# A fused encoder layer on one core: input projections in matmuls of 512 columns, and a last norm that is begun before the last expert's rows are in

## The reference, cut to what matters

```python
h = layer_norm(concat([meta, x]), ln_in_g, ln_in_b)        # 16 + 256 rows of 1024
proj = h @ w_in                  # q 256, k 256, v 512, og 512, a1 16, z 512, xbc 1024, dt 8
# GLA heads on q, k, v; SSD heads on conv(xbc), dt; outputs gated by silu(og), silu(z)
h1 = layer_norm(alpha * h + mix @ w_out, ln1_g, ln1_b)
# 32 experts, top 4 of each token; d_model = d_ff = 1024
hid = clamped_swiglu(xb @ w_gate[e] + b_gate[e], xb @ w_up[e] + b_up[e])
yb = (hid @ w_down[e] + b_down[e]) * gate
out = layer_norm(alpha * h1 + segment_sum(yb), ln2_g, ln2_b)   # 256 rows
```

## Time and profile before

| | |
|---|---|
| median of 3 runs | 1058.77 us (1058.34 to 1059.03) |
| the profiled execution | 1058.86 us, span of its instructions 1057.0 us |
| PE busy | 1021.6 us (97%) |
| DMA | 426.21 MB, mean 403 GB/s |
| VectorE, ScalarE, GpSimd busy | 228.6, 143.9, 29.7 us |
| mean granted TensorE clock | 0.991 |

### The profile page before, as it was taken

One profiled execution on the slowest core, in us unless ns is written; L12 is line 12 of the kernel. 1 busy time (PEld: TensorE's weight loads), 2 busy tenths in 40 slices (PEclk: granted clock), 3 DMA queues, 4 the chain that ended last, 5 costly groups with the idle time before them and its releaser, 6 DMA issues.

```text
span 1057.0 us, 12137 instructions
## 1 busy us (share of the span) xinstructions
PE 1021.6 (97%) x5116; PEld 449.5 (43%) x5116; DVE 228.6 (22%) x495; ACT 143.9 (14%) x348; POOL 29.7 (3%) x50
## 2 busy tenths in 40 slices
PE   8999999999999999999999999999999999999997
PEld 7888764333333333333333333333333333333332
DVE  5453572111111111111111112211111111111112
ACT  3312331111111111011110111111111110011102
POOL 1230100000000000000000000000000000000000
PEclk9999999999999999999999999999999999999999
DMA  9894689999999999999999999999999999999995
GB/s 314 273 410 192 201 327 410 428 428 435 429 429 435 432 425 433 435 436 424 430 435 436 424 422 436 432 430 426 435 434 428 428 435 435 430 425 427 428 418 236
DMA packets 40011, 426.21 MB, mean 403 GB/s; under 512 B 6922, under 2 KB 19347, under 8 KB 23204
## 3 DMA queue, kind: packets, MB, share of 16 engines
q1 hardware_dynamic: 37940, 424.12, 95.6%
q10 hardware_dynamic: 2032, 1.53, 0.6%
HBM read 424.59 MB, written 1.05 MB: 403 GB/s over the span
## 4 chain that ended last, share of the span: by engine, by line
PE 72%; DMA 26%; ACT 1%; DVE 0%; issue 0%; SPq 0%; POOL 0%; DVEq 0%; POOLq 0%; ACTq 0%
PE bank L1200 30%; DMA ring<-in_moe_w_up 18%; PE bank L1251 15%; DMA ring<-in_moe_w_gate 8%; PE bank L1180 4%; PE bank L1172 4%; PE bank L856 3%; PE bank L871 2%; PE bank L1046 2%; PE bank L1034 1%; PE bank L988 1%; PE bank L1242 1%; PE bank L1120 1%; PE bank L949 1%; PE bank L1054 1%; PE bank L1220 1%
## 5 line engine op out<-in xcount | busy, mean ns | idle before, releaser
L1200 PE MATMUL bank<-ring,arena 128*64 128x512 f32 x1988 | 447.5, 603 | 23.8 <-DMA ring<-in_moe_w_up 20.3
L1200 PEld LDWEIGHTS bank<-ring,arena 128*64 128x64 f32 x1988 | 142.5, 139 | 298.7 <-issue 257.7
L1251 PE MATMUL bank<-ring,arena 128*64 128x512 f32 x1024 | 226.8, 595 | 1.5 <-issue 1.5
L1251 PEld LDWEIGHTS bank<-ring,arena 128*64 128x64 f32 x1024 | 71.5, 137 | 151.7 <-issue 150.2
L1641 DVE COPY arena<-bank 128x512 f32<-128x512 f32 x32 | 22.1, 692 | 326.0 <-PE bank L1251 326.0
L741 ACT ACTIVATE arena<-arena 128x512 f32<-128x512 f32 x32 | 20.1, 629 | 451.1 <-DVE arena L1628 451.1
L1180 PE MATMUL bank<-arena 64*128 64x512 f32 x256 | 72.0, 640 | 0.9 <-DVE arena L1641 0.9
L1172 PEld LDWEIGHTS bank<-arena 128*128 128x128 f32 x480 | 58.8, 196 | 22.8 <-issue 22.8
L1635 DVE TENSOR_SCALAR arena<-bank 128x512 f32<-128x512 f32 x32 | 22.1, 692 | 210.3 <-PE bank L1200 210.3
L752 ACT ACTIVATE arena<-bank 128x512 f32<-128x512 f32 x32 | 19.1, 597 | 337.4 <-PE bank L1242 337.4
L1172 PE MATMUL bank<-arena 128*128 128x128 f32 x480 | 64.5, 288 | 0.0
(11 more groups left out here) (281 smaller groups left out, 511.6 us busy)
## 6 DMA issues: line engine op xcount, KB each, us to landing
ring<-in_moe_w_down SPq DMA_DIRECT2D x25, 4096.0 KB, 29.6
ring<-in_moe_w_gate SPq DMA_DIRECT2D x24, 4096.0 KB, 25.4
ring<-in_moe_w_up SPq DMA_DIRECT2D x24, 4096.0 KB, 28.2
ring<-in_moe_w_gate SPq DMA_DIRECT2D x10, 2048.0 KB, 22.6
ring<-in_moe_w_up SPq DMA_DIRECT2D x10, 2048.0 KB, 15.2
ring<-in_moe_w_down SPq DMA_DIRECT2D x10, 2048.0 KB, 17.4
ring<-in_w_in SPq DMA_DIRECT2D x12, 1024.0 KB, 11.8
ring<-in_moe_w_gate SPq DMA_DIRECT2D x8, 1024.0 KB, 17.2
```

What stands on the lines that cost most here:

```text
L1200: ins = mm(b[h * SL:(h + 1) * SL, :], (xA[pp], xB)[q][:, k, par * SL:(par + 1) * SL], columns(unit_at(m, kt), h), start=False, stop=kt == ...
L1251: ins = mm(bank[6][h * SL:(h + 1) * SL, :], hidT[:, kt % 4, (kt // 4) * SL:(kt // 4 + 1) * SL], unit_at(2, kt)[:, h * 512:(h + 1) * 512], ...
```

## The change

**Mixer.** The ring places of the two V units, the two Z units and the two OG units are used as one block of 512 columns each (`w_wide`). The first DMA of a pair now brings the row groups 0 to 3 of all 512 columns, the second the row groups 4 to 7. PE makes V, Z and OG in matmuls of 512 columns, one token tile after the other (`token_wide`). The small products among V's stand after half of a token tile, the `mix_y` transposes after three quarters of OG, as before. Four semaphores are merged into others (`dt_ps`, `dt_ok`, `la_ps`).

**Tile 0.** `counts` goes to free columns of bank 7, so that PE waits for `list_ok` only before the gather. VectorE makes the list after the first clamp. The transposes of the gates move from expert 0 to expert 3, and the first bias product of the gate bank moves behind the first gather.

**The end has two forms**, chosen by `nx` on ScalarE, PE and VectorE. With `nx` = 0: ScalarE sums the four banks before expert 31's rows are in (`early_sums`), and GpSimd makes the early means. VectorE, which waits for `ln2_in` before it copies the last down product, multiplies `ln2_g` by the root of D; the copy (now a TENSOR_SCALAR) also sums each row of `y_s` (`ysum`). PE scatters tile 0, forms the change of the mean as a product of the scatter table with `ysum` (`mean_shift`), and scatters tile 1. ScalarE takes the squares about the early mean for all four banks; GpSimd subtracts the square of the shift; VectorE centres with the true mean. `keep_clock` and bn_stats are gone. The other form (`nx` above 0) does the same after the loop, with a zero `ysum`.

```diff
+BIASED = UNROLL - 1
+WIDE = (U_V, U_Z, U_OG)
...
+        def w_wide(n):
+            return ring[:, n // 4, (n % 4) * HW:(n % 4 + 2) * HW].rearrange("p (k n) -> p k n", k=KT)
...
             for n, c0 in enumerate(W_ORDER):
-                sp.dma_start(w_unit(n), w_in[0, :, c0:c0 + 256].rearrange("(k p) n -> p k n", p=P)).then_inc(w_landed[n], 16)
+                if n in WIDE or n - 1 in WIDE:
+                    u = n if n in WIDE else n - 1
+                    c0, rows = W_ORDER[u], HALVES[n - u]
+                    sp.dma_start(w_wide(u)[:, rows, :], w_in[0, :, c0:c0 + 512].rearrange("(k p) n -> p k n", p=P)[:, rows, :]).then_inc(
+                        w_landed[n], 16)
+                else:
+                    sp.dma_start(w_unit(n), w_in[0, :, c0:c0 + 256].rearrange("(k p) n -> p k n", p=P)).then_inc(w_landed[n], 16)
...
+            pool.wait_ge(ssq, 3)
+            by_half = sums.rearrange("p (t h) -> p t h", h=2)
+            link(nc.gpsimd.tensor_tensor(mean0, by_half[:, :, 0], by_half[:, :, 1], ALU.add))
+            nc.gpsimd.tensor_scalar(nmean0, mean0, -1.0, None, ALU.mult).then_inc(nmean_ok, 1)
             pool.wait_ge(var2, 1)
-            link(root(rstd[:, 0:1], vtmp[:, 0:1], P))
-            nc.gpsimd.tensor_scalar(diag[:, :], ident[:, :], rstd[:, 0:1], None, ALU.mult).then_inc(diag_ok, 1)
-            pool.wait_ge(ssq, 3)
-            link(nc.gpsimd.tensor_scalar(vtmp[:, 1:2], sso[:, 4:5], 1.0 / D, LN_EPS, ALU.mult, ALU.add))
-            root(rstd[:, 1:2], vtmp[:, 1:2], P).then_inc(rstd2, 1)
+            link(nc.gpsimd.tensor_tensor(shift2, shift, shift, ALU.mult))
+            for t in range(NT):
+                pool.wait_ge(ssq, 5 + 2 * t)
+                sq0, sq1, v = squares[:, 2 * t:2 * t + 1], squares[:, 2 * t + 1:2 * t + 2], vtmp[:, t:t + 1]
+                link(nc.gpsimd.tensor_scalar(v, sq0, sq1, LN_EPS * D, ALU.add, ALU.add))
+                link(nc.gpsimd.tensor_tensor(v, v, shift2[:, t:t + 1], ALU.subtract))
+                root(rstd[:, t:t + 1], vtmp[:, t:t + 1], P).then_inc(rstd2, 1)
+                if t == 0:
+                    pool.wait_ge(rstd2, 1)
+                    nc.gpsimd.tensor_scalar(diag[:, :], ident[:, :], rstd[:, 0:1], None, ALU.mult).then_inc(diag_ok, 1)
...
-                if first:
+                if isinstance(n, int) and n == BIASED:
...
+            def early_sums(scattered):
+                nc.scalar.preload_act_table_set("natural_log_exp_and_others")
+                act.wait_ge(scat[1], scattered)
+                for n in range(4):
+                    ins = nc.scalar.activation(scratch[n], bank[n][:, :], ACT.Identity, scale=1.0 / D, accum_out=sums[:, n:n + 1])
+                ins.then_inc(ssq, 1)
+            def output_norm():
+                act.wait_ge(nmean_ok, 2)
+                for n in range(4):
+                    act.wait_ge(last_ps, n + 1)
+                    nc.scalar.activation(scratch[4 + n], bank[n][:, :], ACT.Square, bias=nmean0[:, n // 2:n // 2 + 1],
+                                         accum_out=squares[:, n:n + 1]).then_inc(ssq, 1)
+                for h in range(2):
+                    act.wait_ge(fin_ps, h + 1)
+                    nc.scalar.activation(z2[:, 0, h * 512:(h + 1) * 512], bank[4 + h][:, :], ACT.Copy).then_inc(fin0, 1)
+                act.wait_ge(fin0, 2)
+                act.dma_start(out[0, 0:P, 512:D], z2[:, 0, 512:D]).then_inc(out_done, 16)
+                act.wait_ge(out_done, 16 * 2 * NT)
+            with act.If(nx < 1):
+                early_sums(NE - 1)
+                output_norm()
...
-            nc.scalar.preload_act_table_set("natural_log_exp_and_others")
-            act.wait_ge(scat[1], nx + NE)
...
-            mean_part(0)
-            link(mean_part(1))
-            nc.scalar.activation(nmean, sso[:, 0:1], ACT.Identity, bias=sso[:, 1:2]).then_inc(nmean_ok, 1)
-            act.wait_ge(nmean_ok, 2)
-            square_part(0)
-            link(square_part(1))
-            nc.scalar.activation(sso[:, 4:5], sso[:, 2:3], ACT.Identity, bias=sso[:, 3:4]).then_inc(ssq, 1)
...
+            def token_wide(out, n, t, kts):
+                for kt in kts:
+                    if kt % 4 == 0:
+                        pe.wait_ge(w_landed[n + kt // 4], 16)
+                    ins = mm(out, hT[:, kt, META + t * P:META + (t + 1) * P], w_wide(n)[:, kt, :], start=kt == 0, stop=kt == KT - 1)
+                return ins
...
-            pe.wait_ge(w_landed[U_V], 16)
             pe.wait_ge(conv, 8)
             pe.wait_ge(cT_ok, 6)
-            token_major(bank[5][:, 0:256], U_V, 0)
-
-            pe.wait_ge(dt_ok, 1)
+            token_wide(bank[5][:, :], U_V, 0, first_half)
+
+            pe.wait_ge(dt_ok, 2)
...
-            token_major(bank[7][:, 0:256], U_V, 1)
+            token_wide(bank[5][:, :], U_V, 0, second_half).then_inc(v_ps, 1)
             pe.wait_ge(la_ok, 1)
...
-            ins.then_inc(D_ps, 1)
-            pe.wait_ge(w_landed[U_V + 1], 16)
-            for t, b in enumerate((bank[5], bank[7])):
-                token_major(b[:, 256:512], U_V + 1, t).then_inc(v_ps, 1)
-            meta_rows(bank[3][:, 0:HV], HV, [(U_V + g // 2, (g % 2) * HV) for g in range(4)]).then_inc(v_ps, 1)
+            ins.then_inc(la_ps, 1)
+            token_wide(bank[7][:, :], U_V, 1, range(KT)).then_inc(v_ps, 1)
+            meta_rows(bank[3][:, 0:HV], HV, w_wide(U_V)).then_inc(v_ps, 1)
...
             pe.wait_ge(q_ok, 1)
...
+            for t in range(NT):
+                token_wide(bank[(0, 5)[t]][:, :], U_Z, t, range(KT)).then_inc(z_ps, 1)
...
-                        pe.wait_ge(mix_y, 2)
-                        mix_transposes(bank[0], z_t, (4, 5))
-                        mix_transposes(bank[5], z_t, (6, 7))
+            token_wide(bank[6][:, :], U_OG, 0, range(KT)).then_inc(og_ps, 1)
+            token_wide(bank[7][:, :], U_OG, 1, first_half)
+            pe.wait_ge(mix_y, 2)
+            mix_transposes(bank[0], z_t, (4, 5))
+            mix_transposes(bank[5], z_t, (6, 7))
+            token_wide(bank[7][:, :], U_OG, 1, second_half).then_inc(og_ps, 1)
...
-            hidden_bias(0, bank[4], 0, True)
...
                 gather_part(1, half, banks).then_inc(gath_ps, 1)
+            hidden_bias(0, bank[4], 0, True)
...
-                    ins = mm(bank[5][0:1, 0:NE], ones_b[:, 0:1], maskb[:, t, :], start=t == 0, stop=t == 1)
+                    ins = mm(bank[7][0:1, SEQ:SEQ + NE], ones_b[:, 0:1], maskb[:, t, :], start=t == 0, stop=t == 1)
...
                 if first:
                     counts()
+                listing = isinstance(n, int) and n == BIASED
+                if listing:
                     gate_transposes()
-                else:
+                if not first:
                     pe.wait_ge(yd_ok, n)
                 pe.wait_ge(selG_ok, n + 1)
                 for t in range(NT):
                     ins = tr(bank[6][:, t * P:(t + 1) * P], selG[:, par, t, :], ident[:, :])
                 ins.then_inc(selT_ps, 1)
-                if first:
-                    pe.wait_ge(list_ok, 1)
                 last = isinstance(n, int) and n == NE - 1
                 if last:
                     scatter(n - 1, 0, 1 - par)
...
                 if scatters and not last:
                     scatter(n - 1, 0, 1 - par)
                 if first:
+                    pe.wait_ge(list_ok, 1)
+                if listing:
                     pe.wait_ge(GT_ok, 1)
...
-            for t in range(NT):
-                scatter(NE - 1, t, 1)
...
+            def mean_shift(done, count):
+                for t in range(NT):
+                    ins = mm(bank[7][:, t:t + 1], selGT[1][:, t * P:(t + 1) * P], ysum, start=True, stop=True)
+                ins.then_inc(done, count)
+            def last_scatter(t, h):
+                mm(bank[2 * t + h][:, :], selGT[1][h * SL:(h + 1) * SL, t * P:(t + 1) * P], y_s[h * SL:(h + 1) * SL, :],
+                   start=False, stop=False, skip_group_check=True).then_inc(last_ps, 1)
+            def output_norm():
+                pe.wait_ge(ln2_in, 32)
+                for h in range(2):
+                    mm(bank[4 + h][:, :], ones[0:1, :], lnbc[0:1, 1, h * 512:(h + 1) * 512], start=True, stop=False)
+                pe.wait_ge(diag_ok, 1)
+                for h in range(2):
+                    pe.wait_ge(cen, 2 * NT + h + 1)
+                    mm(bank[4 + h][:, :], diag[:, :], z2[:, 0, h * 512:(h + 1) * 512], start=False, stop=True).then_inc(fin_ps, 1)
+            with pe.If(nx < 1):
+                pe.wait_ge(yd_ok, NE)
+                pe.wait_ge(ssq, 3)
+                for h in range(2):
+                    last_scatter(0, h)
+                mean_shift(shift_ps, 1)
+                for h in range(2):
+                    last_scatter(1, h)
+                output_norm()
...
-            keep_clock(bank[7], 5)
...
+            def list_overflow():
...
```

(77 more changed lines are left out.)

91 lines of the change are left out of this document (28 added, 63 removed).

## The result

The changed kernel takes 1063.76 us (median of 13 runs), the one before 1058.90 (13 runs beside it): ratio 1.0049, 95% interval 1.0036 to 1.0062. The forecast was 1059.1 in a range of 1056.8 to 1061.3. The profiled execution took 1064.28, its span is 1062.5 against 1057.0. One of the 13 runs before took 5250.7 us, and one of the 13 after 1073.28 at a mean granted clock of 0.944; no trace of either was kept, and the medians don't hang on them.

What follows compares the result with a forecast made beforehand. PE's chain was taken to bound the kernel up to the mixer's end, then the experts' DMA bytes. -1.0 + 1.91 - 0.7 + 0.15 = +0.36 on 1058.86 gave 1059.2, the median 0.09 lower: 1059.1, range 1056.8 to 1061.3.

Steps and rivals of the forecast that it cites:

- Mixer: V, Z and OG in products of 512 columns: PE reaches the experts' stage sooner, -1.0 us.
- Tile 0: PE's wait for the list goes, PE gains 1.0 us beside the busy DMA stream: worth 0.
- The stream: Experts' loads: same bytes, same order; ln2_b last, landing 18.9 us after issue, behind the down product's end.
- The new wait: VectorE waits for ln2_in and multiplies before the last down product's copy, making it late: +1.91 us.
- Rival A: At the end, the ln2 wait costs nothing as its loads land before the down product ends: 1057.2; chance 0.12.
- The rest of the tail: From the last copy's end through scatter and new norm to the output: shorter, -0.7 us.
- rival B: At the end, PE's clock falls in the wait's 2.8 us gap: +2.2 us in all, 1061.3; chance 0.14.
- The branch: Jump over the unused form at the end: 0 to 0.4 us, taken as +0.15.

Runs made afterwards that it cites:

- E13: E1 with the second form of the end left out on PE alone: 1059.91 us, ratio 1.0008.
- E11: The changed kernel with the second form of the end left out on ScalarE, PE and VectorE: 1063.75 us, ratio 1.0044.
- E15: E11 with nine clock keepers filling the gap ahead of PE's wait for the last copy: 1061.28 us, ratio 1.0023.
- E12: E1 with the second form of the end left out on ScalarE, PE and VectorE: 1058.57 us, ratio 0.9998.
- E1: The changed kernel with VectorE's wait for ln2_in and the multiplication moved behind the last copy: 1061.45 us, ratio 1.0023.
- E3: The kernel before with only the mixer's products of 512 columns: 1063.45 us, ratio 1.0041.
- E9: E3 with 48 short products at the start in place of four clock keepers, shifting PE's code back: 1059.54 us, ratio 1.0008.
- E7: E6 with the two forms swapped, so that the executed form lies behind a jump: 1067.26 us, ratio 1.0072.
- E6: E1 with five clock keepers ahead of PE's wait for diag_ok: 1061.75 us, ratio 1.0025.
- E14: E1 with the second form of the end left out on ScalarE alone: 1060.65 us, ratio 1.0012.
- E4: The kernel before with a wait for ln2_in and a multiplication by 1.0 ahead of the last copy: 1062.49 us, ratio 1.0037.
- E10: The kernel before with 16 short products at the start and one clock keeper fewer, shifting PE's code: 1062.87 us, ratio 1.0044.
- E2: The changed kernel with nine clock keepers filling the gap ahead of PE's wait for the last copy: 1063.77 us, ratio 1.0047.

## Why the prediction was wrong

**Mixer, -1.0: mis-sized.** It measured 0.26: the out products start at 117.65 instead of 117.91. Z lost 32 records and 0.08 us, OG's first stretch 24 records and 0.06 us: 2.5 ns for each. The stream's last load is issued 0.44 us sooner; where the other 0.2 comes from is not shown, and the last down product starts anywhere from 1037.4 to 1038.3 in the profiles of these kernels. I divided the length of a run of products by their number (218.9 ns for 256 columns) and took the difference to 429.4 as the price of a record. But the length has a fixed part, in the narrow and the wide form alike: 14.01 = 64 x 0.2159 + 0.19, 13.93 = 32 x 0.4294 + 0.19, 10.50 = 24 x 0.4294 + 0.19. L1046's 6.87 = 16 x 0.4294 has none, so I compared lengths with it and without it, and V's 14.20 counted it twice over. The Trainium skill (TensorE: Matmul & The Clock Gate, Part 1) gave 96 x 2.5 ns = 0.24 us; the measurement sides with it.

**Tile 0: right.** The wait is gone, PE's up product ends 1 us sooner, and the stream behind shows none of it.

**The stream: right.** `ln2_b` took 18.8 us from issue to landing, as before, and was still behind the down product.

**The new wait, +1.91: right.** 1.77 measured; the multiplication took 0.69 where I took 0.81. Rival A is out.

**The rest of the tail, -0.7: wrong even at full clock.** E13 shows it with the clock at 1.00 throughout. From the copy's end at 1045.65, its timeline:

```profile
1048.90 0.31 POOL L570 TENSOR_SCALAR small<-small 128x1 f32<-128x1 f32 x1 [0.55 <-ACT arena L810]
...
1050.24 0.63 POOL L575 TENSOR_SCALAR tri<-ident,small 128x128 f32<-128x128 f32 x1
...
1050.92 1.98 PE L1361 MATMUL bank<-arena,tri 128*128 128x512 f32 x4 [0.58 <-POOL tri L575]
```

`diag` is ready at +5.2 and not +4.6: GpSimd began its first small operation (L570) 0.47 us after it was let go, a hand-over that I had at a few hundredths, and that operation took 0.31 us where I took 0.19. ScalarE's last copy ends at +7.9 (predicted +7.2, before +7.71), VectorE's end is +7.95 (predicted +7.15, before +8.09). The new norm is no shorter than the old.

**The step that failed: rival B's price, and its chance of 0.14.** The mechanism came as written, gap and all. But I let the low clock cost only until the last root, +2.2, as if the products behind it didn't count. It stayed at 1.2 GHz for ten microseconds, so L1357 and L1361 took 1.8 us more each as well, and the chain that ended last is PE's. From the copy's end to PE's last product the changed kernel needs 11.48 us and E13, whose clock stayed at 1.00 up to there, needs 7.25: the low clock is 4.2 us of the profiled execution. Not all of that is the gap's, since the clock can fall without it; filling the gap was worth 2.5 (E11 to E15). Wait and second form together account for the loss: with both out (E12) the kernel is level with the one before. The mean granted clock is 0.984 to 0.987 in 12 of the changed kernel's 13 runs (0.988 to 0.993 in 90 of 91 runs of the kernel before that stood beside the experiments), so 0.14 was also too little a chance: I had taken one row of the clock's fall for an edge that the gap would mostly pass.

**The branch, 0.15 (0 to 0.4): too low, and for a reason that I had not seen.** It measured 0.55 in the profile, all of it behind the last byte, in ScalarE's jump over its unused form; E11's median, uncertain by a microsecond, doesn't show it. And it hides more: once the wait is moved, the same second form costs 2.9 us (E1 to E12). Half of that I put down to PE's block of code, which then comes in the store and not ahead of it. In the changed kernel that block comes at 1056.8, before the store begins at 1058.2, and E11, without the form, is no faster. This is why the causes don't add up one by one.

**What the prediction never considered: where the code lies.** The mixer alone, forecast at -1.0, is +4.8 (E3), and E9, level with the kernel before, shows that this is not the mixer's products. In the changed kernel this stop does not occur, because the executed form comes ahead of the jump (E7 puts it back). So it explains nothing of the 4.9 us; but with the mixer's part applied alone one would have blamed the products.

**What stays open.** Why the clock falls at 1049.0 in one kernel, at 1051.6 in another and only behind the last product in a third with the same work before it (E6, E1, E13), and so whether a filler that holds it exists; the 0.5 us between E12 and the sum of E13 and E14; and 1.1 us of E15's 2.7 beyond what E4's profile gave the late copy.

## What to carry to other kernels

Look at the end of a kernel as its own stage: a load that is waited for one step too early there costs its own lateness and then the clock of every product behind it, so price a low clock to the last product, not to the next wait. Put the multiplication behind the copy that others wait for; that edit alone took back 2.3 of the 4.9 us, and 5.2 where the second form was out (E11 to E12). Before believing a small change in a program with jumps, compare the same kernel with its code shifted by a few dozen instructions: here that alone moved the time by 0.4%.

## What was unexpected of the hardware

- A jump over code that isn't run can stop TensorE for 2.0 to 3.0 us (E10 1.98, E7 3.03) with nothing to wait for in the profile; whether it does depends on how many instructions lie ahead of it in the program (E10: about 64 more, +4.1 us). In the profile it is an idle time with releaser "issue" just behind a 16 KB packet of queue q8.
- At the end of a program the same jump on ScalarE comes behind the last byte: 1.4 us to the span's end instead of 0.85 (E13 against E12).
- A 16 KB block of code that comes in the middle of a store goes with a trail of 2 KB pieces on one of 16 DMA engines, some 1.5 us long (E1, E14; 1.1 us in E2). Without a block the trail was 0.4 us in E13; that the block makes it is not shown.
- With a gap of 2.58 us ahead of the last products the granted clock fell and then stayed at 1.2 GHz under 10 us of uninterrupted products (the changed kernel); with 2.71 us it did not fall before the store (E4's profile); with rests of at most 0.9 us it fell in seven profiles, and in four only during the store or behind it.
